# Two-block transformer on one core: the chunked recurrence's TensorE and VectorE order, and when the first expert weights are loaded

## The reference, cut to what matters

```python
xs = tuple(jnp.moveaxis(t, 1, 0) for t in (rh, kh, vh, dh, a_vec, b_vec))
_, y = lax.scan(step, jnp.zeros((B, H, N, N), jnp.float32), xs)
y = head_norm(y, gn_gain.reshape(H, N), RWKV_GN_EPS)
...
mixed = jnp.concatenate([ret, rw], axis=-1).astype(x.dtype)
h = h + mixed @ w_out[l]
h = h + hier_moe(rms_norm_2(h, norm2_gain[l]), w_route_group[l], b_route_group[l], w_route_expert[l], b_route_expert[l], w_gate[l], w_up[l], w_down[l])
...
hdn = jax.nn.silu(xblk @ w_gate[e]) * (xblk @ w_up[e])
return hdn @ w_down[e]
```

## Times and profile before

| | us |
|---|---|
| median of 3 runs | 1007.21 |
| lowest and highest | 1005.79, 1007.43 |
| the profiled execution, own time | 1006.36 |
| its span in the profile | 1004.2 |
| PE busy | 874.0 (87%) |
| DVE busy | 447.9 (45%) |
| ACT busy | 331.9 (33%) |
| HBM read | 290.25 MB, 293 GB/s over the span |

### The profile page before, as it was taken

How to read it: one execution, slowest core, us unless ns; L and a number is a source line. 1 busy time by engine, 2 the same in 40 slices (tenths; PEclk the granted TensorE clock), 3 DMA queues, 4 the chain that set the end, 5 groups by cost and what they waited for, 6 DMA issues and landing times.

```text
span 1004.2 us, 16158 instructions
## 1 busy us (share of the span) xinstructions
PE 874.0 (87%) x6998; PEld 604.3 (60%) x6998; DVE 447.9 (45%) x578; ACT 331.9 (33%) x433; POOL 22.0 (2%) x35
## 2 busy tenths in 40 slices
PE   9999999999999999999989988767867775786785
PEld 7889988888888889989979533211312221131232
DVE  6776878677876448898756310000100010010011
ACT  6476664665555328644523300000000000000002
POOL 0420000000000000000100000000000000000000
PEclk9999999999999999999999998787888898798898
DMA  9893325576645546352369999999999999999995
GB/s 323 256 358 131 144 86 168 168 250 208 208 169 179 198 155 222 131 205 85 109 186 386 373 415 403 429 427 428 428 429 428 428 428 428 428 428 428 424 426 221
DMA packets 75968, 294.34 MB, mean 293 GB/s; under 512 B 5247, under 2 KB 32655, under 8 KB 62592
## 3 DMA queue, kind: packets, MB, share of 16 engines
q1 hardware_dynamic: 70352, 283.91, 72.6%
q10 hardware_dynamic: 4128, 6.34, 1.8%
q0 software_dynamic: 1424, 3.16, 1.1%
HBM read 290.25 MB, written 4.10 MB: 293 GB/s over the span
## 4 chain that ended last, share of the span: by engine, by line
PE 64%; DMA 27%; DVE 5%; issue 1%; SPq 1%; ACT 1%; DVEq 0%; ACTq 0%
DMA arena<-in_w_down 10%; DMA arena<-in_w_gate 9%; DMA arena<-in_w_up 9%; PE psum L1271 8%; PE psum L1960 7%; PE psum L1134 6%; PE psum L1136 6%; PE psum L1135 6%; PE psum L1298 4%; PE psum L1273 4%; PE psum L1988 4%; PE psum L1635 2%; PE psum L1941 2%; PE psum L1171 1%; PE psum L1170 1%; PE psum L1168 1%
## 5 line engine op out<-in xcount | busy, mean ns | idle before, releaser
L1960 PE MATMUL psum<-arena,featL 128*32 128x512 f32 x1008 | 158.6, 696 | 61.0 <-DMA arena<-in_w_up 35.1
L2543 DVE TENSOR_TENSOR ring_rounded<-arena,hi_rounded 128x2048 fp32r<-128x2048 f32 x75 | 171.3, 2289 | 60.6 <-ACT hi_rounded L2087 59.3
L2087 ACT ACTIVATE hi_rounded<-arena 128x2048 fp32r<-128x2048 f32 x76 | 144.8, 1912 | 85.9 <-DMA arena<-in_w_down 18.0
L1960 PEld LDWEIGHTS psum<-arena,featL 128*32 128x32 f32 x1008 | 38.1, 124 | 169.2 <-issue 86.3
L1271 PE MATMUL psum<-ffn_in_rounded,hi_rounded 128*128 128x512 f32 x352 | 122.6, 395 | 0.7 <-DVE ffn_in_rounded L2535 0.7
L1988 PE MATMUL psum<-arena,featT 128*32 128x512 f32 x424 | 78.0, 733 | 35.5 <-DMA arena<-in_w_down 31.2
L1134 PE MATMUL psum<-hi_rounded,featT_rounded 128*128 128x256 f32 (+1 forms) x336 | 104.1, 310 | 0.8 <-DVE ring_rounded L2543 0.7
L1136 PE MATMUL psum<-hi_rounded,featL_rounded 128*128 128x256 f32 (+1 forms) x336 | 101.8, 303 | 0.0
L1135 PE MATMUL psum<-ring_rounded,featT_rounded 128*128 128x256 f32 (+1 forms) x336 | 101.8, 303 | 0.0
L1273 PE MATMUL psum<-ffn_in_rounded,ring_rounded 128*128 128x256 f32 x352 | 97.6, 277 | 0.0
L1271 PEld LDWEIGHTS psum<-ffn_in_rounded,hi_rounded 128*128 128x128 f32 x352 | 66.0, 188 | 16.2 <-DVE ffn_in_rounded L2535 1.0
(11 more groups left out here) (369 smaller groups left out, 1284.6 us busy)
## 6 DMA issues: line engine op xcount, KB each, us to landing
arena<-in_w_down SPq DMA_DIRECT2D x32, 2048.0 KB, 17.1
arena<-in_w_gate SPq DMA_DIRECT2D x28, 2048.0 KB, 20.6
arena<-in_w_up SPq DMA_DIRECT2D x24, 2048.0 KB, 24.1
arena<-in_w_in SPq DMA_DIRECT2D x14, 2048.0 KB, 8.9
arena<-in_w_up SPq DMA_DIRECT2D x25, 1024.0 KB, 9.0
arena<-in_w_gate SPq DMA_DIRECT2D x14, 1024.0 KB, 5.6
arena<-in_w_down SPq DMA_DIRECT2D x7, 1024.0 KB, 10.4
arena<-in_w_out SPq DMA_DIRECT2D x3, 2048.0 KB, 8.1
```

The lines of the kernel that those rows point to most:

```text
L1960: ins = mm(psum[32 * j:32 * j + 32, MB[4 + m], :], xg[:, 4 * half + k, 32 * j:32 * j + 32], weights(m, half, j, 512 * k), start=half == 0 ...
L2087: fn(high, view, ACT.Copy).then_inc(hi_ready, 1)
L2543: tt(low, view, high.bitcast(F32), ALU.subtract).then_inc(lo_ready, 1)
```

## The change

Three things are changed. PE's order in the recurrence: the turn mT(0, 0) goes from behind u_state(1) to behind u_inner(0), u_inner(3) takes its place, the output rows of tile 0 go ahead of state(2), and in tile 1 the state's part of chunk 3 alternates with the rows' part of chunk 2. VectorE's order: the low part of mT(0, 0) and the first gain go into the wait for state(0), and y_gain(0) and rw_scale(0) go to later places; ScalarE's y_squares(0) goes behind the last U. SyncE's: the cells' parts no longer wait one by one.

```diff
         if c == 0:
+            add("dve", "mT", 0, 0)
             for half in range(2):
                 add("act", "WT", half)
-        if c == 1:
-            add("dve", "mT", 0, 0)
         if c < NCH - 1:
             add("dve", "St", c)
-        if c == 2:
-            for who, par in Y_EMPTIED:
-                add(who, "Y", 0, par)
+    for who, par in Y_EMPTIED:
+        add(who, "Y", 0, par)
     for who, par in Y_EMPTIED:
         add(who, "Y", 1, par)
     add("dve", "mT", 1, 0)
...
-                 3: (final_gain, late[:], spent[:, LE["GT"][0]:LE["gap"][1]])}
+                 3: (row("ret_gn"), late[:], row("rw_gn"), spent[:, LE["GT"][0]:LE["gap"][1]])}
...
                     wait_filled(sp, "ro", NT - 1)
-                    first_load(2, 0, ("mat", "A", 1), ("natl", "V", 1), ("vraw", 1, 1), *inv(("P2", 1)))
-                    first_load(2, 1, *inv(("P3", 1), ("P4T", 1), ("H1", 0), ("H1", 1)))
+                    first_load(2, 0)
+                    wait_filled(sp, "inv", "P2", 1)
+                    first_load(2, 1)
+                    wait_filled(sp, "inv", "P4T", 1)
+                    wait_emptied(sp, "mat", "A", 1)
+                    first_load(NQ + 2, 3, hi=2)
                     wait_emptied(sp, "mat", "Aak", 1)
-                    first_load(NQ, 0, ("gn", 1), ("inv", "N", 1), ("mat", "Ro", 1), ("inv", "HT", 1))
-                    first_load(3, 3, *inv(("G1", 0), ("G1", 1), ("G2", 0), ("G2", 1)))
+                    wait_filled(sp, "mat", "Re", 0)
+                    first_load(NQ, 0)
+                    wait_filled(sp, "inv", "HT", 0)
+                    first_load(3, 3)
                     sp.wait_ge(mixed_ready, 1)
-                    first_load(2, 2, *inv(("TT", 0), ("TT", 1)), ("Q", 0), ("Q", 1))
-                    first_load(NQ, 1, ("U", 0, 1), ("WT", 0), ("WT", 1), ("St", 0))
-                    first_load(3, 2, ("U", 1, 1), ("St", 1), ("U", 2, 1), ("St", 2))
+                    wait_filled(sp, "inv", "G2", 0)
+                    first_load(2, 2)
+                    wait_filled(sp, "Q", 0)
+                    first_load(NQ, 1)
+                    wait_filled(sp, "WT", 1)
+                    first_load(3, 2)
                     wait_emptied(sp, "U", 1, 0)
-                    first_load(NQ + 2, 3, hi=2)
+                    first_load(NQ + 2, 3, lo=2, hi=3)
                     sp.wait_ge(mixed_ready, NT)
                     sp.wait_ge(u_first, NCH - 1)
                     first_load(2, 3)
...
+                    first_load(NQ + 2, 3, lo=3)
                     first_load(0, 1)
                     first_load(0, 2)
...
-            def y_state(banks, c, opens):
-
-                t = c // 2
+            def y_state(banks, c):
...
-            def y_rows(banks, *chunks):
+                        y_from_state(banks, c, i, par)
+
+            def y_from_state(banks, c, i, par):
+
+                r = head_rows(par)
+                ins = mm(banks[par][head_rows(c % 2), 64 * i:64 * i + 64], f_r[r, i, tokens(c // 2, c % 2)], S[c][r, i, :],
+                         start=i == 0, stop=False, skip_group_check=True)
+                if i == 3:
+                    ins.then_inc(y_first, 1)
+                return ins
+
+            def y_known(c):
 
                 for name in ("Re", "Ro"):
                     wait_emptied(pe, "mat", name, 1)
-                for c in chunks:
-                    u_known(c)
-                    if c:
-                        pe.wait_ge(y_first, 2 * c)
-                for i in range(4):
-                    for par in range(2):
-                        for c in chunks:
-                            t, both, h = c // 2, (Re, Ro)[c % 2], 2 * i + par
-                            ins = mm(banks[par][head_rows(c % 2), 64 * i:64 * i + 64], both[:, t, 4 * par + i, :],
-                                     VU[c][:, 64 * h:64 * h + 64], start=c == 0 and i == 0, stop=True, skip_group_check=True)
-                            if c % 2 and i == 3:
-                                end(ins)
+                u_known(c)
+                if c:
+                    pe.wait_ge(y_first, 2 * c)
+
+            def y_from_rows(banks, c, i, par):
+
+                t, both, h = c // 2, (Re, Ro)[c % 2], 2 * i + par
+                return mm(banks[par][head_rows(c % 2), 64 * i:64 * i + 64], both[:, t, 4 * par + i, :],
+                          VU[c][:, 64 * h:64 * h + 64], start=c == 0 and i == 0, stop=True, skip_group_check=True)
 
             u_inner(0)
+            transposes(("mT", 0, 0), mixed_rows(0, 0), lambda: pe.wait_ge(mixed_ready, 1))
             banks = [begin("WT", c).rearrange("p (t i q) -> p t i q", t=NT, i=4) for c in range(2)]
             wait_emptied(pe, "inv", "TT", NT - 1)
             wait_emptied(pe, "natl", "A", 1)
...
             state(0)
             u1, u2 = u_inner(1, 2)
             u_state(u1, 1)
-            transposes(("mT", 0, 0), mixed_rows(0, 0), lambda: pe.wait_ge(mixed_ready, 1))
+            u3, = u_inner(3)
             state(1)
             y0 = [begin("Y", 0, par) for par in range(2)]
-            y_state(y0, 1, True)
+            y_state(y0, 1)
             u_state(u2, 2)
-            u3, = u_inner(3)
+            for c in range(2):
+                y_known(c)
+            for i in range(4):
+                for par in range(2):
+                    for c in range(2):
+                        y_from_rows(y0, c, i, par)
             state(2)
-            y_rows(y0, 0, 1)
+            y1 = [begin("Y", 1, par) for par in range(2)]
+            y_state(y1, 2)
             u_state(u3, 3)
-            y1 = [begin("Y", 1, par) for par in range(2)]
-            y_state(y1, 2, True)
-            y_state(y1, 3, True)
-            y_rows(y1, 2)
-            y_rows(y1, 3)
+            y_known(2)
+            for i in range(4):
+                for par in range(2):
+                    ins = y_from_state(y1, 3, i, par)
+                    if i == 0:
+                        end(ins)
+                    y_from_rows(y1, 2, i, par)
+            y_known(3)
+            for i in range(4):
+                for par in range(2):
+                    ins = y_from_rows(y1, 3, i, par)
+                    if i == 3:
+                        end(ins)
...
             gated_bonus(1)
-            gated_gain(0)
             for c in range(NCH):
                 r = slice(64 * (1 - c % 2), 64 * (1 - c % 2) + 64)
...
                 if c < NCH - 1:
-                    if c == 1:
-                        low_moved("mT", 0, 0)
                     if c:
                         link(tt(S[c + 1], S[c], bc(PC[:, :, c], 64), ALU.mult))
+                    else:
+                        low_moved("mT", 0, 0)
+                        gated_gain(0)
                     wait_filled(dve, "St", c)
                     b = bank("St", c)[:, 0:256].rearrange("p (i v) -> p i v", v=64)
                     if c == 0:
...
                     else:
                         empty(tt(S[c + 1], S[c + 1], b, ALU.add), "St", c)
-                    if c == 2:
-                        y_gain(0)
+            y_gain(0)
             rw_mean(0)
-            rw_scale(0)
             y_gain(1)
             rw_mean(1)
+            rw_scale(0)
             rw_mixed(0)
             low_moved("mT", 1, 0)
             rw_scale(1)
```

More of the change, by code:

```diff
@@ L965, in moe_stream @@
                     first_load(NQ + 2, 2)
-                    first_load(NQ + 2, 3, lo=2)
+                    first_load(NQ + 2, 3, lo=3)
                     first_load(0, 1)
@@ L2402, in _ @@
                 if c == 0:
+                    high_moved("mT", 0, 0)
                     for half in range(2):
@@ L2406, in _ @@
                                  bank("WT", half).rearrange("p (t i q) -> p t i q", t=NT, i=4), ACT.Copy), "WT", half)
-                if c == 1:
-                    high_moved("mT", 0, 0)
-                if c == 2:
-                    y_squares(0)
+            y_squares(0)
             root(48, RW_H, 64, 2)
```

5 lines of the change are left out of this document (removed).

## The result

| | before | changed |
|---|---|---|
| median of 18 runs each, us | 1006.11 | 1010.62 |
| lowest and highest | 1003.85, 1007.45 | 1006.88, 1012.93 |
| span of the profiled execution | 1004.2 | 1008.1 |

The ratio is 1.0043, interval 1.0034 to 1.0052: **4.3 us slower** (4.5 between the medians), and the median lies 2.0 us above the top of the range. TensorE is already late at the end of the recurrence. The third projection half tile starts at 539.18 us against 532.70, SyncE issues the gated ring load at 620.50 against 614.85 (its piece in the chain is the 614.96 of the earlier trace rows), and the span ends 3.9 later.

A forecast was written before the change was run, and what follows sets the result against it. TensorE before 530 us was taken to set the 615 us loads and the end, though expert weights pace 620 to 980 us. Terms -0.3 (parts 1 to 4), -0.1 (part 5), -1.2 (part 6) gave -1.6: 1005.6 us, range 1004.1 to 1008.6.

The forecast's parts named there:

- The frame: TensorE's progress before 530 us sets the loads of 615 us, which wait for their slot, and through them the end.
- One for one: Each microsecond TensorE saves before 530 us moves the loads of 615 us, and the end, by one microsecond.
- Early weights count for nothing: Weights loaded earlier without TensorE being earlier move nothing; 1.75 MB coming earlier counted for nothing.
- Parts 1, 2 and 4: Recurrence: turn moved (cost 0.12 us), VectorE's sum earlier (-1.0), VectorE's tail ending at 532.25 (TensorE waits 1.2); parts 1 to 4: -0.3.
- part 2: State 1: VectorE no longer moves turned rows there, so its sum ends at 521.97 instead of 523.01: -1.0 us.
- Part 3: Tile 0's output rows ahead of state(2), outer and inner products alternating: mT(1,0) turned near 527.9, not 529.34; no further gain.
- Part 5: SyncE issues four loads together behind one wait; only their effect on instruction fetches counts: 0 to -0.2 us.
- bad bound of +1.5: Bursts delay the fetches at the borders of 502.2, 506.8 and 511.3 us by 1.1 each, the first having slack: +1.5 us.
- Rival C: Bursts make three fetches between 502 and 511 us 1.1 us late and the clock falls: +1.2 us, 1008.4; chance 0.13.
- Part 6: TensorE's clock stays full after 513.4:516.8 us, as the turns raise busy time to about 2.0 us: -1.2 us.

The follow-up runs named there:

- second profiles: The kernel before and the changed kernel, both unchanged, profiled a second time; third half tile starts at 532.85 us before, 539.12 changed.
- y_blocks: The changed kernel with tile 1's output products in two blocks of 16 records instead of alternated; ratio 1.0025 to the kernel before.
- burst_all: order_blocks with all seven cells of quarters loaded in bursts, parts of cell (NQ+2,3) left as before; ratio 1.0035 to the kernel before.
- late_22: order_blocks with the loads of cell (2,2), 1 MB, moved behind cell (NQ,1), and (3,2) behind them; ratio 0.9980 to the kernel before.
- late_both: order_blocks with VectorE's low part of mT(1,0) before tile 0's scale and mix, and cells (3,3) and (2,2), 2 MB, loaded later; ratio 0.9987 to the kernel before.
- order_blocks: The changed kernel with tile 1's products in blocks and the loads of the kernel before; ratio 0.9993 to the kernel before.
- turn_back: order_blocks with the turn of mT(0,0) and both halves of its move back at their old places; ratio 1.0012 to the kernel before.
- order_new: The changed order of TensorE, VectorE and ScalarE with the loads of the kernel before; ratio 1.0012 to the kernel before.

## Why the prediction was wrong

**The frame held, within a microsecond or two.** H3 +6.5 (+6.3 in the second profiles), ring load +5.6 (+6.1), spans +3.9 and +6.8, median +4.3. "One for one" is right to within a microsecond up to the ring; the median keeps some 1.3 us less than the ring. The two profiled spans, 3.9 apart, differ there by the clock at the very end: the last but one group of 32 products took 3.30 us in the kernel before and 1.97 in the changed one, both in the chain:

```profile
987.40 3.30 PE psum L1881 x32
```

```profile
992.62 1.97 PE psum L1904 x32
```

That is a draw and no part of the median's difference that is shown: in the second profiles it is the changed kernel that has such a group (988.57, 3.48 us), the kernel before has none, and the spans are 6.8 apart. "Early weights count for nothing" held for the earlier pieces (y_blocks against burst_all) and for 1 MB later (late_22), not for 2 (late_both).

**Parts 1, 2 and 4: right in kind.** No wait for the sum in order_blocks, a new one for the low part of 0.8 us against 1.2. Of itself the wait of part 2 is worth less than my 1.0: turn_back has it at 0.22 us, and the kernel before at 0.5 in its second profile.

**Part 3: the term that was mis-sized.** "With outer and inner products alternating, mT(1,0) is turned near 527.9" took its price from L1731's 32 records in 0.93 us. Those alternate too, but two products of one depth. Here a 64-row product follows a 128-row one: 14 changes more than in blocks, 2.7 us, and H3 3.1 us later (order_new against order_blocks). No rival held it, since I looked for waits and a change of shape is none. The rows of the page had both shapes in plain sight, 64*64 for L1714 and 128*64 for L1731.

**Part 5: the step that failed.** It put the bursts at 0 to -0.2 us; they cost 5.5 us at H3 (the change against order_new). I reasoned from the delay of 2.6 us at a load share of 93.1% and took that as the loaded case. But share is not depth. There a quarter or two was outstanding, behind the bursts three or four, and the fetch waited up to 4.4 us. My bad bound of +1.5 counted three fetches 1.1 us late; the one behind border 32 was 2.7 late, and 2.9 in the second profile. I had one burst of 1 MB near each border, and two stood back to back ahead of the first. The stalls from 500 to 520 us were 3.7 us in the change against 0.9 in order_new, which has its order; the other 2.6 of the 5.5 I put down to the two stretches at half clock, of which order_new has none; they were not measured apart. Rival C was this mechanism with its place and its point of decision right (a fetch longer than the 4.5 us between two borders), and it had 0.13 and 1.2 us.

The page "DMA: Bandwidth & Descriptors" of the Trainium skill, on arbitration, was cited in the prediction for the view that four loads delay a fetch no more than one: the runs speak against that here. So they do against the view of "Runtime: NRT & Kernel Launch", section "Instruction fetch mechanics", that crossing a border is mostly hidden: from 500 to 520 us it cost 1.3 us in order_blocks and 3.7 in the change. It was hidden where no load moved (late_both).

**Part 6: right sum, wrong use.** I put PE's busy time in the stretch with the turn at 2.0 us; it was 1.97, and the clock fell. It stayed only where the stall was shorter as well. The -1.2 was conditional on part 5, and I added them as if they were independent: with the bursts it turned into a second stretch at half clock (in the first profile; the second has one stretch, and longer stalls).

Together: forecast -1.6. order_blocks, which is the forecast without its two errors, reached -2.0 at H3 and 0.9993 of the time, within its interval the same as before.

## What to carry to other kernels

Ahead of TensorE's page borders count what is outstanding on the DMA queues, not only how busy they are; where a page lasts only 4 to 5 us, loads of 256 KB go out one by one, or elsewhere. Before products are interleaved to fill waits, compare their tile shapes: two shapes cost a fixed time at each change, one shape in different output halves is a gain. And when an edit's gain hangs on another's (here the clock on the stall), price the pair.

## What the runs showed of the hardware that I had not expected

- A change between products of 64 and 128 rows of depth costs 0.18 to 0.19 us on TensorE; 64-row products in different row halves, or 128-row ones into different output halves, follow each other at 0.03 to 0.04 us a record (32 in 0.93 to 1.15 us), 128-row ones into one half at 0.06 (32 in 1.83).
- With no load moving, the instruction fetch began 0.7 and 0.8 us behind its border (late_both, borders 34 and 33), and 1.8 where the fetch before was late (late_22, border 34). No fetch began less than 2.39 us behind the landing of the one before. With quarters issued one by one it began 0.8 to 3.3 us behind its border, with two cells back to back up to 4.4.
- The releaser that the profile names can be wrong at a border: ScalarE was named for 2.0 us that were a missing page.
